# One level of Strassen for the projections of a two-branch token mixer on one TensorE

## The chip, the core and the metric

The kernel runs on one core of a Trainium2 chip, which has five engines with queues of their own: TensorE (PE, matrix products), VectorE (DVE), ScalarE (ACT), GpSimd (POOL) and SyncE (SP, which here only issues transfers). The metric is the device time of one execution in microseconds (us), the median over the runs.

## What is computed

One layer over 1024 tokens of width 1024, all in float32:

```python
h = rms_norm(x, pre_norm)
q, k, v, gate_a, u_b, v_b, gate_b, mg_a, mg_b = split(h @ w_in)   # 1024, 128, 128, then six of 1024 columns
o_a = sliding_window_attention(q, k, v, sinks, rel_bias)          # window 128, 16 heads, 2 K/V heads
y_a = (o_a * silu(gate_a)) @ w_branch_a
o_b = spatial_gating(gelu(u_b), gelu(v_b), ...)                   # layer norm of v, then tril(W) over chunks of 128
y_b = (o_b * silu(gate_b)) @ w_branch_b
merged = sigmoid(mg_a) * y_a + sigmoid(mg_b) * y_b
x = x + rms_norm(merged @ w_out, post_norm)
```

## The kernel before

**Products.** Every operand of a large product is held as a high part (rounded to the reduced float32 format fp32r, by ScalarE) and a low part (the rest, by a subtraction on GpSimd or VectorE). A product is the sum of three: high x high, high x low, low x high. `products` (from L460) lists them for one unit: 8 slabs of depth, 3 combinations, 2 halves of 512 columns, so 48 matmuls of 128x512, all issued at L474. A unit yields 128 output rows (features) x 1024 tokens in one of the two accumulators acc0 and acc1 (two PSUM banks each).

**Stages.** (1) The V branch: eight tiles of tokens; x is normalised, transposed, split and multiplied by the 1024 columns of v_b; GELU, layer norm and the chunk mix (L501, L503) follow, and mix_b goes to memory. h itself, transposed and split, is gathered in ht_hi and ht_lo. (2) U and gate_b, 16 units in turn, whose results make g_hi and g_lo. (3) merge gate B and branch B, 16 units. (4) K and V. (5) Attention: for each of eight head pairs the units gate_a, merge gate A and the next Q (144 matmuls) run, and `beside` puts a slot of attention work between them after every 11 matmuls (FIRST_SLOT, SLOT_STEP): scores of block k (L600), transpose of the probabilities of block k-2 (L612), values of block k-4 (L627). (6) Branch A, 8 units, with the merge. (7) The output: 8 tiles of tokens x 2 halves x 24 matmuls (L694), then the post norm, x added, and the store.

**What sets the order.** Each engine has its program in one written order, with semaphores between them. Loads of weight slabs are issued by SP (`load_raw`, L293) once the slab before the last is split; ScalarE makes w_hi (`split_hi`, L735), GpSimd w_lo (`split_lo`, L1015), and the unit waits for it. In attention VectorE takes for block k: masked copy of the scores (L1351), maxima over scores plus bias (L1357), the negated maximum and the sink's difference (L1363, L1364); ScalarE takes the exponentials (L912, L914); VectorE the denominator (L1339, L1340); GpSimd scales the probabilities (L1113) and masks their transposes (L1123). GpSimd also writes the bias row (L1092), which SP stores to memory and spreads to skew_d.

Of the kernel before, what the change touches and what calls it, by code (L numbers as in the profile page):

```python
# [5 lines left out]
P = 128  # L31
D_MODEL = 1024
SEQ = 1024
# [11 lines left out]
PAIRS = N_HEADS // 2  # L45
PAIRS_PER_KV = PAIRS // N_KV


# [11 lines left out]
N_U = NT  # L60
N_MB = N_U + 2 * KT
N_KVU = N_MB + 2 * KT
N_ATT = N_KVU + 2
N_YA = N_ATT + 3 * PAIRS
N_OUT = N_YA + KT
BIAS_ROW = 3 * P
WARM_UP = 24
UNIT = 6 * KT


FIRST_SLOT, SLOT_STEP, SLOTS = 19, 11, NT + 4
# [12 lines left out]
class Chain:  # L84


    def __init__(self, eng, sem):
        self.eng, self.sem, self.base, self.k = eng, sem, 0, 0

    def link(self, ins):  # L90
        self.k += 1
        ins.then_inc(self.sem, 1)
        self.eng.wait_ge(self.sem, self.base + self.k)

    def at(self, base):
        self.base, self.k = base, 0


def build(nc, x, rel_bias, pre_norm, post_norm, w_in, sinks, sgu_ln_g, sgu_ln_b,
          w_spatial, b_spatial, w_branch_a, w_branch_b, w_out, out):  # L100
    f32 = mybir.dt.float32
    f32r = mybir.dt.float32r
    bf16 = mybir.dt.bfloat16
# [8 lines left out]

    mix_d = nc.dram_tensor("mix_d", [KT, P, SEQ], f32)
    acc_d = nc.dram_tensor("acc_d", [KT, P, SEQ], f32)
    sig_d = nc.dram_tensor("sig_d", [KT, P, SEQ], f32)
# [3 lines left out]
    with ExitStack() as ctx:  # L119
# [6 lines left out]

        ht_hi = sb("ht_hi", [P, KT * SEQ], f32r)
        ht_lo = sb("ht_lo", [P, KT * SEQ], f32r)
        g_hi = sb("g_hi", [P, KT * SEQ], f32r)
        g_lo = sb("g_lo", [P, KT * SEQ], f32r)  # L130
        raw = [sb(f"raw{b}", [P, 1024]) for b in range(2)]
        w_hi = [sb(f"w_hi{b}", [P, 1024], f32r) for b in range(2)]
        w_lo = [sb(f"w_lo{b}", [P, 1024], f32r) for b in range(2)]
        buf_t = sb("buf_t", [P, SEQ])
        buf_a = sb("buf_a", [P, SEQ])
        buf_b = sb("buf_b", [P, SEQ])
        junk = sb("junk", [P, SEQ], bf16)
# [21 lines left out]
        bias_row = sb("bias_row", [N_HEADS, BIAS_ROW])  # L159


        with ExitStack() as s0:
            x_b = [sb(f"x_b{b}", [P, D_MODEL], f32, s0) for b in range(2)]
            pre_b = sb("pre_b", [P, D_MODEL], f32, s0)
            lng_b = sb("lng_b", [P, D_MODEL], f32, s0)
            lnb_b = sb("lnb_b", [P, D_MODEL], f32, s0)
            bs_b = sb("bs_b", [P, KT * P], f32, s0)
            mix_b = [sb(f"mix_b{b}", [P, KT * P], f32, s0) for b in range(2)]
            vn_hi = sb("vn_hi", [P, D_MODEL], f32r, s0)
            vn_lo = sb("vn_lo", [P, D_MODEL], f32r, s0)  # L170
            ws_st = sb("ws_st", [P, KT * 2 * P], f32r, s0)
        with ExitStack() as s1:
            k_hi = sb("k_hi", [P, N_KV * SEQ], f32r, s1)
            k_lo = sb("k_lo", [P, N_KV * SEQ], f32r, s1)
            v_st = sb("v_st", [P, N_KV * NT * P], f32r, s1)
            q_st = [sb(f"q_st{h}", [P, SEQ], f32r, s1) for h in range(2)]


            prob = [sb(f"prob{b}", [P, 256], f32, s1) for b in range(3)]
            pt_packed = sb("pt_packed", [P, 512], f32r, s1)  # L180
            pt = [sb(f"pt{b}", [P, 1024], f32r, s1) for b in range(2)]
            bias_t = sb("bias_t", [P, 512], f32, s1)
            bias_p = sb("bias_p", [P, 256], f32, s1)
            o_tmp = [sb(f"o_tmp{b}", [P, 256], f32, s1) for b in range(2)]
        with ExitStack() as s2:
            wo_hi = sb("wo_hi", [P, KT * HALF], f32r, s2)
            wo_lo = sb("wo_lo", [P, KT * HALF], f32r, s2)
            x_r = [sb(f"x_r{b}", [P, D_MODEL], f32, s2) for b in range(2)]
# [4 lines left out]
        ps_s, ps_p = ps_t[:, 0:512], ps_t[:, 512:768]  # L193

        raw_in = [sem(f"raw_in{b}") for b in range(2)]
        hi_done, lo_done = sem("hi_done"), sem("lo_done")
        unit_done = sem("unit_done")
        acc_free = [sem(f"acc_free{b}") for b in range(2)]  # L200
        x_in = [sem(f"x_in{b}") for b in range(2)]
        pre_in, ln_in, bs_in, wsp_in = sem("pre_in"), sem("ln_in"), sem("bs_in"), sem("wsp_in")
        rel_in, sink_in, bias_out, skew_out = sem("rel_in"), sem("sink_in"), sem("bias_out"), sem("skew_out")
        bias_made = sem("bias_made")
        const_ok, wsp_ok = sem("const_ok"), sem("wsp_ok")
        ssq_ok, msq_ok, rstd_ok, h_ok = sem("ssq_ok"), sem("msq_ok"), sem("rstd_ok"), sem("h_ok")
        tr_done = sem("tr_done")
        hs_hi, hs_lo = sem("hs_hi"), sem("hs_lo")
        ht_in = [sem(f"ht_in{b}") for b in range(2)]
        vb_in = [sem(f"vb_in{b}") for b in range(4)]  # L210
        vb_lo_dve, vb_lo_pool = sem("vb_lo_dve"), sem("vb_lo_pool")
        wsh_ok, wsl_ok = sem("wsh_ok"), sem("wsl_ok")
        var_ok, lnr_ok, vn_ok = sem("var_ok"), sem("lnr_ok"), sem("vn_ok")
        vnh_ok, vnl_ok = sem("vnh_ok"), sem("vnl_ok")
        mix_done, mix_lo_out, mix_ok, mix_biased = sem("mix_done"), sem("mix_lo_out"), sem("mix_ok"), sem("mix_biased")
        mix_out = [sem(f"mix_out{b}") for b in range(2)]
        mix_in, gate_t_ok, um_ok, prod_ok = sem("mix_in"), sem("gate_t_ok"), sem("um_ok"), sem("prod_ok")
        ghi_ok, g_ready = sem("ghi_ok"), sem("g_ready")
        spill_out = sem("spill_out")
        khi_ok, klo_ok, vt_done, vhi_ok = sem("khi_ok"), sem("klo_ok"), sem("vt_done"), sem("vhi_ok")  # L220
        bias_in, before_ok = sem("bias_in"), sem("before_ok")
        q_hi_ok = sem("q_hi_ok")
# [4 lines left out]
        pt_done, pth_ok, ptl_ok, pt_ok, pv_done = (  # L227
            sem("pt_done"), sem("pth_ok"), sem("ptl_ok"), sem("pt_ok"), sem("pv_done"))

        otmp_ok, oadd_ok, gtan_ok, og_ok = (  # L230
            sem("otmp_ok"), sem("oadd_ok"), sem("gtan_ok"), sem("og_ok"))
        siga_ok = sem("siga_ok")

        sigr_in, accr_in, mrg_ok, mhi_ok = sem("sigr_in"), sem("accr_in"), sem("mrg_ok"), sem("mhi_ok")
        post_in, xr_in = sem("post_in"), [sem(f"xr_in{b}") for b in range(2)]
        mt_hi, mt_lo = sem("mt_hi"), sem("mt_lo")

        osq_ok, oms_ok, ors_ok, y_ok = sem("osq_ok"), sem("oms_ok"), sem("ors_ok"), sem("y_ok")
# [29 lines left out]

        def wo_land(s):
            return raw[s % 2] if s < 6 else x_r[s % 2]  # L270

        def wait_wo(eng, s):

            if s in (5, 7):
                eng.wait_ge(wo_lo_dve, 1 if s == 5 else 2)
            else:
                eng.wait_ge(lo_done, N_OUT + (s if s < 5 else 5) + 1)

        def wait_vb_lo(eng, k):

            if k in vb_by_pool:
# [1222 lines left out]
```

## Time and profile before

| | us |
|---|---|
| median of 3 runs (1043.58 to 1044.3) | 1044.2 |
| span of the profiled execution | 1041.6 |
| TensorE busy | 1014.4 (97%) |
| VectorE, ScalarE, GpSimd busy | 459.4, 343.1, 402.0 |
| mean granted clock of TensorE | 0.995 |

The profile shows one execution on the chip. "Busy" is the time in which an engine worked on an instruction. PE is TensorE's matmuls, PEld its loads of the stationary operand, which run beside them. In a group of instructions "out<-in" names the tiles, "xcount" how many there are, then the busy time in us, the mean ns of one, and the idle time of the engine just before them with its releaser. Matmuls overlap in the pipeline, so their pace is read from the distance between starts, not from the duration of one. In rows cut into 40 slices each digit is tenths of a slice.

### The profile page before, as it was taken

The numbers are of one execution on the slowest core, as the hardware profiler recorded it, in microseconds if no ns is written. First come the engines' busy times: TensorE is split into PE (matmuls) and PEld (weight loads), VectorE is DVE, ScalarE is ACT, GpSimd is POOL, SyncE is SP. The second block draws the span as 40 slices with busy tenths as digits, with TensorE's granted clock in tenths as the row PEclk, the third lists the DMA queues.
The fourth block names the chain that finished last, engine by engine and source line by source line (L and its number), as shares of the span: only waits on it lengthen the run. The fifth ranks groups of instructions, "written<-read, shape, count | busy, mean of one in ns | idle before, by whom it ended". The sixth has DMA issues, their size and how long they took to land.

```text
span 1041.6 us, 14172 instructions
## 1 busy us (share of the span) xinstructions
PE 1014.4 (97%) x4792; PEld 840.5 (81%) x4792; DVE 459.4 (44%) x975; ACT 343.1 (33%) x716; POOL 402.0 (39%) x426
## 2 busy tenths in 40 slices
PE   7999999999999999999999999999999999999997
PEld 6888887888888888888877878787787878888886
DVE  6777633322331010011465566656556664335323
ACT  5333322212221111112354455455444533223221
POOL 2244545211212222122256656565565663224000
PEclk8999999999999999999999999999999999999999
DMA  9844242232531212212111112111111213455322
GB/s 314 230 143 141 84 133 87 69 92 60 154 89 60 81 60 92 69 60 81 31 52 62 52 40 70 40 53 49 61 51 41 71 42 101 163 212 174 137 81 81
DMA packets 113028, 98.03 MB, mean 94 GB/s; under 512 B 3664, under 2 KB 100960, under 8 KB 112992
## 3 DMA queue, kind: packets, MB, share of 16 engines
q1 hardware_dynamic: 108384, 80.79, 25.7%
q10 hardware_dynamic: 4608, 16.78, 4.2%
q8 instruction: 21, 0.34, 0.2%
q14 instruction: 15, 0.12, 0.0%
HBM read 72.36 MB, written 19.95 MB: 89 GB/s over the span
## 4 chain that ended last, share of the span: by engine, by line
PE 61%; DVE 13%; issue 13%; ACT 7%; POOL 3%; DMA 2%; DVEq 0%; ACTq 0%; SPq 0%; POOLq 0%
PE acc L474 56%; DVE neg_max L1363 3%; ACT prob L912 3%; DVE prob L1357 3%; DVE ps_t L1351 2%; PE ps_m L627 1%; DMA raw<-in_w_in 1%; DVE denom L1339 1%; ACT pt_packed L895 1%; ACT w_hi L875 1%; POOL bias_row L1092 1%; ACT buf_t L885 1%; ACT q_st L856 1%; PE ps_t L600 1%; DVE q_st L1318 1%
## 5 line engine op out<-in xcount | busy, mean ns | idle before, releaser
L1015 POOL TENSOR_TENSOR w_lo<-raw,w_hi 128x1024 fp32r<-128x1024 f32 x66 | 159.1, 2411 | 314.0 <-ACT w_hi L735 313.0
L474 PE MATMUL acc<-ht_hi,w_hi 128*128 128x512 f32 x800 | 250.7, 391 | 1.6 <-POOL w_lo L1015 1.6
L474 PE MATMUL acc<-ht_hi,w_lo 128*128 128x512 f32 x800 | 250.9, 392 | 0.0
L474 PE MATMUL acc<-ht_lo,w_hi 128*128 128x512 f32 x800 | 249.7, 390 | 0.0
L474 PEld LDWEIGHTS acc<-ht_hi,w_hi 128*128 128x128 f32 x800 | 149.1, 188 | 31.0 <-issue 2.0
L474 PEld LDWEIGHTS acc<-ht_lo,w_hi 128*128 128x128 f32 x800 | 149.4, 188 | 29.2
L474 PEld LDWEIGHTS acc<-ht_hi,w_lo 128*128 128x128 f32 x800 | 149.3, 188 | 29.2
L474 PE MATMUL acc<-g_hi,w_hi 128*128 128x512 f32 x384 | 120.3, 395 | 0.9 <-DVE w_lo L1192 0.5
L474 PE MATMUL acc<-g_lo,w_hi 128*128 128x512 f32 x384 | 119.4, 392 | 0.0
L474 PE MATMUL acc<-g_hi,w_lo 128*128 128x512 f32 x384 | 118.9, 391 | 0.0
L912 ACT ACTIVATE prob<-prob,neg_max 128x128 f32<-128x128 f32 x128 | 50.5, 395 | 151.6 <-DVE sink_d L1364 151.6
L735 ACT ACTIVATE w_hi<-raw 128x1024 fp32r<-128x1024 f32 x58 | 61.3, 1057 | 90.0 <-PE acc L474 78.5
L1113 POOL TENSOR_SCALAR prob<-prob,inv_den 128x128 f32<-128x128 f32 x128 | 46.0, 372 | 114.0 <-DVE inv_den L1340 114.0
L474 PEld LDWEIGHTS acc<-g_hi,w_hi 128*128 128x128 f32 x384 | 71.1, 189 | 17.8 <-DVE w_lo L1192 1.9
L474 PEld LDWEIGHTS acc<-g_hi,w_lo 128*128 128x128 f32 x384 | 72.1, 188 | 15.0
L474 PEld LDWEIGHTS acc<-g_lo,w_hi 128*128 128x128 f32 x384 | 71.9, 189 | 14.7
L1123 POOL TENSOR_SCALAR_AFFINE_SELECT pt<-pt_packed 128x512 fp32r<-128x512 f32 x120 | 73.5, 635 | 9.3 <-DVE pt_packed L1343 7.7
L600 PE MATMUL ps_t<-k_hi,q_st 128*128 128x256 f32 (+1 forms) x128 | 37.4, 315 | 6.0 <-DVE row_max L1357 5.1
L1363 DVE TENSOR_SCALAR neg_max<-row_max 128x2 f32<-128x2 f32 x64 | 41.2, 644 | 2.2
L1292 DVE TENSOR_TENSOR buf_a<-acc,buf_t 128x1024 f32<-128x1024 f32 x8 | 9.8, 1225 | 73.2 <-PE acc L474 73.2
L627 PEld LDWEIGHTS ps_m<-pt,v_st 128*128 128x128 f32 x240 | 37.6, 190 | 5.5
L1339 DVE TENSOR_TENSOR denom<-row_sum,sink_e 128x2 f32<-128x2 f32 x64 | 19.2, 300 | 50.9 <-ACT sink_e L914 50.9
(155 smaller groups left out, 1272.0 us busy)
## 6 DMA issues: line engine op xcount, KB each, us to landing
raw<-in_w_in SPq DMA_DIRECT2D x54, 512.0 KB, 3.8
x_b<-in_x SPq DMA_DIRECT2D x8, 512.0 KB, 5.1
ht_hi<-w_hi SPq DMA_DIRECT2D x8, 512.0 KB, 3.8
ht_lo<-w_lo SPq DMA_DIRECT2D x8, 512.0 KB, 4.8
mix_d<-mix_b SPq DMA_DIRECT2D x8, 512.0 KB, 3.3
buf_b<-mix_d SPq DMA_DIRECT2D x8, 512.0 KB, 3.3
raw<-in_w_branch_b SPq DMA_DIRECT2D x8, 512.0 KB, 3.5
acc_d<-buf_a ACTq DMA_DIRECT2D x8, 512.0 KB, 2.6
```

Of the source, the lines that this page charges most:

```text
L474: last = nc.tensor.matmul(o, l, r, start=a, stop=z, skip_group_check=True)
L600: last = nc.tensor.matmul(ps_s[:, h * 256 + lo:(h + 1) * 256], q_st[h][:, blk * P:(blk + 1) * P], kbuf[:, kc + lo:kc + 256], start=a, stop ...
L627: last = nc.tensor.matmul(o, v_st[:, v0:v0 + P], pt[blk % 2][:, c0:c0 + 256].rearrange("p (h c) -> p h c", h=2), start=(kb == kbs[0] and x ...
L735: nc.scalar.activation(w_hi[b][:, :] if dst is None else dst, raw[b][:, :], ACT.Copy).then_inc(hi_done, 1)
L912: nc.scalar.activation(w, w, ACT.Exp, bias=neg_max[:, 2 * k + h:2 * k + h + 1], accum_out=row_sum[:, 2 * k + h:2 * k + h + 1])
L1015: nc.gpsimd.tensor_tensor(w_lo[b][:, :], raw[b][:, :], w_hi[b][:, :].bitcast(f32), ALU.subtract).then_inc(lo_done, 1)
L1113: last = nc.gpsimd.tensor_scalar(w, w, inv_den[:, 2 * k - 2 + h:2 * k - 1 + h], 0.5, ALU.mult, ALU.mult)
L1123: last = nc.gpsimd.affine_select(out=pt[blk % 2][:, kb * 512:(kb + 1) * 512].rearrange("p (y q) -> p y q", y=4), in_=pt_packed[:, :].rearr ...
L1339: own.link(nc.vector.tensor_tensor(denom[:, m2], row_sum[:, m2], sink_e[:, m2], ALU.add))
L1351: own.link(nc.vector.copy_predicated(blocks(ps_s)[:, :, 1, :], heads(before_i), blocks(ps_s)[:, :, 0, :]))
L1357: last = nc.vector.tensor_tensor_reduce(out=prob[k % 3][:, cs], in0=ps_s[:, h * 256 + P:(h + 1) * 256], in1=bias, scale=HEAD_DIM ** -0.5, ...
L1363: nc.vector.tensor_scalar(neg_max[:, c2], row_max[:, c2], -1.0, None, ALU.mult)
```

## The change

The units of (2), (3) but branch B, and (5) become pairs: two slabs of 128 weight columns against all of h, as a 2x2 block product in Winograd's form of Strassen's scheme, seven products of 12 matmuls (4 slabs of depth x 3 combinations, 128x512) instead of eight. Branch B, branch A and the output projection come last, as whole 1024x1024 products in the same scheme, seven products of four units of 12 matmuls each. In outline:

- The sums of h for the scheme are made once behind the V branch (`t_sums`, `t_hi`, `t_lo`): h is kept in memory as ht_d, reloaded by halves, summed on VectorE, split by ScalarE and by GpSimd or VectorE, into `mv`, seven operands with high and low part. The third product of the first pair is the first to read them.
- For each pair VectorE makes four sums of the weights (`left_sums_1`, `left_sums_2`), ScalarE and GpSimd split 3584 columns in four parts instead of 2048, ScalarE evicts three partial results and VectorE adds three from PSUM (`c_11`, `c_22`, `c_21`); products 6, 5 and 3 go on in the bank of product 1, product 4 in that of 7, so they wait for the eviction before them.
- 24 pairs in this order: Q with gate_a and the two merge gates, by turns, 16 in all; then U with gate_b, 8. Attention of a head pair is spread over 14 products of two pairs, one slot in the middle of each product. Transposes come at slot k+3 and values at k+5. The values take the masked transposes of the block before against differences of V (`v_lo`, `pt_prev`), so GpSimd masks one tile per block and not two.
- K and V take their time from two banks behind the V branch, K goes to memory and half of it comes back for each K/V head. The LN gain and bias are folded into later steps (`row_weights`, `u_mix`).
- The squares: ScalarE makes the high parts of 128x2048 for both sides, GpSimd the left low part, VectorE the right low part, the sums and the results (`square`), with buffers for two operands of each side. The merge of the branches is on GpSimd, inside the square of branch B; the output's norm and x are done by rows of 128 while products 6, 5 and 3 of the last square run.

The diff, cut to what the prediction speaks of:

```diff
-        def unit(n, hn, b, rh, rl):
-            start_unit(n, hn, b)
-            run(products(b, w_hi[b], w_lo[b], rh, rl)).then_inc(unit_done, 1)
+FIRST_U, PAIRS = 16, 24
+STEPS = (2, 6, 7, 5, 1, 3, 4)
+ORDER = (1, 2, 7, 4, 6, 5, 3)
+def attention_at(n, s):
+    if not 1 <= n <= FIRST_U:
+        return None
+    return (n - 1) // 2, s + (0 if n % 2 else 7)
...
+# TensorE: one product of a pair
+for m in range(first, last):
+    k, y = m // 3, m % 3
+    ins = nc.tensor.matmul(bank, (w_lo if y == 2 else w_hi)[:, left + k * P:left + (k + 1) * P],
+                           right[:, (OPW if y == 1 else 0) + k * HALF:(OPW if y == 1 else 0) + (k + 1) * HALF],
+                           start=(m == 0 and x in (1, 2, 7)), stop=(m == 11), skip_group_check=True)
...
+# TensorE: a unit of a square
+if i == 0:
+    pe.wait_ge(ll_ok, f + 1)
+    pe.wait_ge(rl_ok, f + 1)
+if x == 7:
+    pe.wait_ge(c_ok, 12 * st + i + 1)
+if x == 4:
+    pe.wait_ge(p7_ok, 4 * st + i + 1)
...
+# VectorE, behind the V branch
+t_sums(0)
+ln_stats(NT - 1)
+ln_apply(NT - 1)
+mix_read(NT - 2)
+t_sums(1)          # waits for bias_out
+t_lo(1)
+nc.vector.tensor_tensor(k_tmp[1], acc[0], k_tmp[0], ALU.subtract)
+mix_read(NT - 1)
+t_sums(2)
+t_sums(3)
+t_lo(3)
+left_sums_1(0)
+left_sums_2(0)
...
+# VectorE, after slot s of pair n
+if s == 0:
+    c_11(n)
+    if n and kind(n - 1) == "Q":
+        gate_mul(n - 1, 0)
+if s == 1:
+    left_sums_1(n + 1)
+if s == 2:
+    left_sums_2(n + 1)
+if s == 3:
+    c_22(n)
...
+# VectorE, a square
+sum_t3(st)
+sum_t1(st)
+right_lo_square(f + 2)
+result(st, 11, 0)
+sum_t2(st)
+result(st, 11, 1)
+sum_t4(st)
+result(st, 11, 2)
+result(st, 11, 3)
...
+right_lo_square(f + 3)
...
+# GpSimd, the squares
+for f in range(21):
+    st, x = f // 7, ORDER[f % 7]
+    if 1 <= f < 20:
+        left_lo_square(f + 1)
+    for i in range(4):
+        if st == BRANCH_B and x in (2, 6, 5, 3):
+            merge({2: 11, 6: 21, 5: 22, 3: 12}[x], i)
...
+# SP, behind the V branch
+sp.wait_ge(bias_out, 16)
+sp.dma_start(skew_d[:, :, :], bass.AP(bias_d, 0, [[BIAS_ROW, N_HEADS], [0, P], [1, BIAS_ROW]]))
+sp.wait_ge(khi_ok, 1)
+sp.dma_start(k_d[0, :, :], k_tmp[0][:, :].bitcast(i32))
+spill_mix(NT - 1)
+load_pair(0, 0)    # waits for t_sums(2)
```

## Rows read from the trace of the kernel before

**Rows 1.** The page: busy us by engine, and TensorE's clock in 40 slices.

```profile
PE 1014.4 (97%) x4792; PEld 840.5 (81%) x4792; DVE 459.4 (44%) x975; ACT 343.1 (33%) x716; POOL 402.0 (39%) x426
...
PEclk8999999999999999999999999999999999999999
```

**Rows 2.** Groups of TensorE's large matmuls.

```profile
L474 PE MATMUL acc<-ht_hi,w_hi 128*128 128x512 f32 x800 | 250.7, 391 | 1.6 <-POOL w_lo L1015 1.6
...
L474 PE MATMUL acc<-g_lo,w_hi 128*128 128x512 f32 x384 | 119.4, 392 | 0.0
L694 PE MATMUL acc<-g_hi,w_hi 128*128 128x512 f32 x128 | 39.6, 391 | 0.0
...
L694 PE MATMUL acc<-wo_hi,w_hi 128*128 128x512 f32 x64 | 25.5, 398 | 0.0
```

**Rows 3.** Timeline of TensorE: start us, us, engine, line, operation, tiles.

```profile
399.99 0.62 PE L474 MATMUL acc<-g_lo,w_hi 128*128 128x512 f32 x2
...
409.51 0.62 PE L474 MATMUL acc<-g_lo,w_hi 128*128 128x512 f32 x2
...
1002.39 0.40 PE L694 MATMUL acc<-wo_hi,w_hi 128*128 128x512 f32 x1
...
1005.89 0.40 PE L694 MATMUL acc<-wo_hi,w_hi 128*128 128x512 f32 x1
```

**Rows 4.** Timeline at the end: the last matmul and the last store.

```profile
1035.36 0.39 PE L694 MATMUL acc<-g_hi,w_lo 128*128 128x512 f32 x1
...
1038.45 0.99 SPq L443 DMA_DIRECT2D out<-buf_b  x2
```

**Rows 5.** Windows: length, busy us (and instructions) by engine, clock, DMA share, GB/s.

```profile
497.40:947.00 449.60, 436.70 (x2170) 361.88 (x2169) 256.23 (x779) 195.91 (x545) 240.88 (x304) 1.00 0.23 74
```

**Rows 6.** Waits of TensorE's weight loads: us in total, times, longest.

```profile
PEld ps_t L600 <- DVE row_max L1357: 11.7, 24, 0.7
PEld ps_t L612 <- POOL prob L1113: 11.1, 16, 1.3
```

**Rows 7.** Groups of the other engines, by shape.

```profile
L1273 DVE TENSOR_TENSOR buf_a<-buf_a,buf_b 128x1024 f32<-128x1024 f32 x8 | 9.8, 1225 | 33.8 <-ACT buf_a L819 24.7 <-DMA buf_b<-mix_d 9.1
L1198 DVE TENSOR_TENSOR mix_b<-ps_m,mix_b 128x512 f32<-128x512 f32 x8 | 5.5, 691 | 13.3 <-ACT mix_b L757 13.3
L735 ACT ACTIVATE w_hi<-raw 128x1024 fp32r<-128x1024 f32 x58 | 61.3, 1057 | 90.0 <-PE acc L474 78.5 <-issue 10.6 <-DMA raw<-in_w_in 0.6
L875 ACT ACTIVATE w_hi<-raw 128x512 fp32r<-128x512 f32 x16 | 9.9, 616 | 0.0
L1015 POOL TENSOR_TENSOR w_lo<-raw,w_hi 128x1024 fp32r<-128x1024 f32 x66 | 159.1, 2411 | 314.0 <-ACT w_hi L735 313.0
L1363 DVE TENSOR_SCALAR neg_max<-row_max 128x2 f32<-128x2 f32 x64 | 41.2, 644 | 2.2
```

**Rows 8.** Timeline of GpSimd and VectorE where the two overlap.

```profile
878.69 2.40 POOL L1015 TENSOR_TENSOR w_lo<-raw,w_hi 128x1024 fp32r<-128x1024 f32 x1 [9.79 <-ACT w_hi L735]
878.71 1.23 DVE L1411 TENSOR_TENSOR buf_b<-acc,buf_t 128x1024 f32<-128x1024 f32 x1 [4.07 <-DMA buf_t<-sig_d]
...
880.05 2.13 DVE L1414 TENSOR_TENSOR buf_b<-buf_b,buf_a 128x1024 f32<-128x1024 f32 x1
```

**Rows 9.** Timeline of GpSimd, the bias row; then transfers: KB, us to landing.

```profile
158.41 9.92 POOL L1092 TENSOR_SCALAR bias_row<-rel_t 16x1 f32<-16x1 f32 x32
...
skew_d<-bias_d SPq DMA_DIRECT2D x1, 3072.0 KB, 15.7
...
bias_d<-bias_row SPq DMA_DIRECT2D x1, 24.0 KB, 3.0
```

**Rows 10.** Timeline of VectorE, one turn of the attention loop.

```profile
673.68 0.42 DVE L1351 COPY_PREDICATED ps_t<-before,ps_t 128x256 f32<-128x256 int32 x1
...
675.48 0.15 DVE L1364 TENSOR_TENSOR sink_d<-sink_p,row_max 128x2 f32<-128x2 f32 x1
...
676.67 0.16 DVE L1339 TENSOR_TENSOR denom<-row_sum,sink_e 128x2 f32<-128x2 f32 x1 [0.27 <-ACT sink_e L914]
...
677.40 0.42 DVE L1351 COPY_PREDICATED ps_t<-before,ps_t 128x256 f32<-128x256 int32 x1
```

More of the change, by code:

```diff
@@ L57, with phase, unit, kind @@
 MGB_COL = MGA_COL + D_MODEL
[L60 to L71, printed above, removed]
+FIRST_U, PAIRS = 16, 24
+U_ORDER = (0, 4, 1, 5, 2, 6, 3, 7)
+LEFT = {1: 0, 2: 1, 6: 2, 7: 3, 5: 4, 3: 5, 4: 6}
+RIGHT = {1: 0, 2: 1, 6: 2, 7: 3, 5: 4, 4: 5, 3: 6}
+STEPS = (2, 6, 7, 5, 1, 3, 4)
+ORDER = (1, 2, 7, 4, 6, 5, 3)
+BRANCH_A, BRANCH_B, OUTPUT = 0, 1, 2
+def phase(st, x):
+    return 7 * st + ORDER.index(x)
+def unit(st, x, i):
+    return 4 * phase(st, x) + i + 1
+def kind(n):
+    if n < FIRST_U:
+        return "M" if n % 2 else "Q"
+    return "U"
+def product_counts():
+    order = [(0, 1)]
+    for n in range(PAIRS):
+        order += [(n, 2), (n, 6), (n, 7), (n, 5)]
+        if n + 1 < PAIRS:
+            order.append((n + 1, 1))
+        order += [(n, 3), (n, 4)]
+    return {key: i + 1 for i, key in enumerate(order)}
+DONE = product_counts()
+def prep_counts():
+    count, out = 0, {}
+    for n in range(PAIRS):
+        for g in ((1, 2), (6, 7), (5, 3), (4,)):
+            count += 1
+            for x in g:
+                out[n, x] = count
+    return out
+SPLIT = prep_counts()
+L_K, L_V, L_T, L_PAIR = 0, 1, 2, 10
+def raw_count(load):
+    return 16 * len(range(load % 3, load + 1, 3))
 def bucket_runs():
@@ L172, in build @@
[L172 to L184, printed above, removed]
@@ L509, in vb_unit @@
+                ins.then_inc(mix_done, 1)
+            def vb_unit(t):
                 pe.wait_ge(hs_lo, t + 1)
[L510 to L521 removed]
@@ new lines, in _ @@
+            for t in range(2, NT):
+                vb_unit(t)
+            pe.wait_ge(kvl_ok, 1)
+            pe.wait_ge(gelu_ok[0], NT // 2)
+            kv_mms(0, k_w, 0, 12)
+            mix(NT - 2)
+            kv_mms(0, k_w, 12, 48).then_inc(k_done, 1)
+            pe.wait_ge(kvl_ok, 2)
+            pe.wait_ge(gelu_ok[1], NT // 2)
+            kv_mms(1, v_w, 0, 12)
+            mix(NT - 1)
+            kv_mms(1, v_w, 12, 48).then_inc(v_done, 1)
+            product(0, 1)
+            product(0, 2)
@@ L688, in out_half @@
-            def out_half(t, b, hf, ks=range(KT), first=False):
-                rh, rl = ((wo_hi, wo_lo) if hf == 0 else (g_hi[:, 0:KT * HALF], g_hi[:, KT * HALF:2 * KT * HALF]))
-                for k in ks:
-                    if first and k % 2 == 0:
-                        wait_wo(pe, 4 * hf + k // 2)
-                    for l, r, kind in ((w_hi[b], rh, 0), (w_hi[b], rl, 1), (w_lo[b], rh, 2)):
-                        last = nc.tensor.matmul(acc[b][:, hf * HALF:(hf + 1) * HALF], l[:, k * P:(k + 1) * P],
-                                                r[:, k * HALF:(k + 1) * HALF], start=(k == 0 and kind == 0),
-                                                stop=(k == KT - 1 and kind == 2), skip_group_check=True)
-                return last
@@ L1485 @@
+            u_gate(PAIRS - 1, 0)
+            for st in range(3):
+                square(st)
 INPUTS = ("x", "rel_bias", "pre_norm", "post_norm", "w_in", "sinks", "sgu_ln_g", "sgu_ln_b", "w_spatial",
```

2487 lines of the change are left out of this document (1488 added, 999 removed).

## Prediction

> **What bounds the kernel now.** I read the page's busy shares first: TensorE is busy for 1014.4 of 1041.6 us, at full clock in nearly every slice [rows 1]. The groups of lines then say with what: 3936 matmuls of 128x512 (800 and 384 in each of three combinations at L474, 384 at L694) [rows 2]. Their pace comes from the timeline: the pair at 399.99 and the pair at 409.51 us lie 42 matmuls apart, 0.2267 us each [rows 3]. 3936 x 0.2267 = 892 us, 86% of the span. The rest is small transposes and mixes, the head, the tail (last matmul issued at about 1035.5 us [rows 4]) and attention. For attention the window from the Q unit to the first output tile holds 449.6 us [rows 5]; it contains 1536 of the large matmuls, 348.2 us, so that attention with its waits costs 101 us. Of this the weight loads stood visibly idle for 22.8 us, waiting for VectorE's row maxima and GpSimd's probabilities [rows 6]. So the kernel is bound by TensorE's work, with one place, attention, where a loop through the other engines is about as long as TensorE's time for a slot.
>
> **What the change takes away.** 48 projection units of 48 matmuls (Q, both branch gates, both merge gates, U: 2304) become 24 pairs of seven products of 12 (2016). The last three projections (1152) become three squares of 7 x 4 x 12 = 336 each (1008). V branch, K and V stay. 3936 - 3504 = 432 matmuls go, 432 x 0.2267 = **97.9 us**. For the pace within a product, which stays in one bank with a new stationary tile each time, there are two rows: wo_hi and wo_lo run at (1005.89 - 1002.39)/15 = 0.233 us, the g_hi half with the same structure at 0.227 by its mean of 391 against 398 ns [rows 2, 3]. I take 0.227, since most groups show it; 0.233 for 3024 product matmuls would cost 20 us. Left alone, the change gives 1041.6 - 97.9 = 943.7 us.
>
> **What it adds on the other engines.** Durations of blocks that no row shows are estimates from two sizes of the same operation [rows 7]. VectorE takes 0.69 us for 512 columns and 1.225 for 1024, so 2.3 for 2048; ScalarE 0.62 and 1.06, so 1.9; GpSimd 2.41 for 1024, so 4.7 for 2048 and 1.25 for 512.
> A row decides how these add up. A GpSimd subtract from SBUF ran from 878.69 to 881.09 us. VectorE's product of acc (PSUM) and buf_t, begun at 878.71, took its usual 1.23; the next, of two SBUF tiles, begun at 880.05, took 2.13 and ended 1.09 after GpSimd let go [rows 8]. So a VectorE operation with two SBUF sources and a GpSimd operation run one after the other, never side by side. The added sums, right splits and gated results are nearly all of this kind. The Trainium skill (SBUF — State Buffer, "SBUF: two separate sides") says the same, that the pair of ports is locked for a whole instruction; by that rule the squares below can't be hidden, and without it my sum would be some 45 us lower; the trace agrees with the rule.
>
> **The seam before the pairs.** TensorE needs the Strassen sums of h for the third product. From the end of the V branch (0): GELU, statistics and the split of the last tile end at about 9.5 us (the copy of the mix stands in ScalarE's queue ahead of it). Then GpSimd writes the bias row, 32 instructions, 9.9 us [rows 9], and its store lands 3.0 us later: 22.4. VectorE's second group of sums waits for that store (t_sums(1), bias_out), and behind it in its queue stand t_lo, the low half of K, the last mix_read and t_sums(2): 2.8 + 1.9 (ScalarE) + 2.3 + 1.2 + 1.4 + 2.8 = 12.4, so 35. Only then is a slab free for the load of pair 0, and SP has put the 3 MB skew, 15.7 us [rows 9], ahead of it: 38 to 41. With ScalarE 1.1 and GpSimd 2.4 the first product starts at about 44, where K, V and two mixes end at 25.7. Some 5 us more go at product 6, which wants all four groups of sums. That is 23; bounds 5 (the bias row early, the skew beside other loads) and 30. I take **20 us**.
>
> **Pairs with attention.** A slot goes from 11 matmuls to 12, 2.72 us, plus 0.5 to 1.2 for attention itself. The loop from one copy_predicated to the next took 677.40 - 673.68 = 3.72 us before [rows 10]: scores, maximum, ScalarE's exponentials, denominator, the next slot. VectorE's queue now gets, between maximum and denominator, c_11 and gate_mul (slot 0), two sums (1, 2), and in slot 3 c_22, which waits for ScalarE's eviction of product 5. The gap there was 1.0 us [rows 10], filled by the exponentials. Two sums need 1.4; slot 3 needs 1.0 + 0.6 + 0.7 = 2.3, so that this loop is 5.0 against TensorE's 3.4. GpSimd has 7168 columns of split per head pair in place of three to five blocks of 1024, and blocks neg_max, whose mean of 644 ns already shows it [rows 7]. I count 1.5 us more waiting per head pair, 8 x 1.5 = **12 us** (-10 if the slot's 0.23 us of additional TensorE time pays for it, +30 if VectorE becomes the bound: of its 256 us in the window [rows 5], with the merges left out, 28 fall to a head pair, and 11 more come, 39 in TensorE's 48, most of it in the first of the two pairs). The U pairs hold 16.6 us of two-source and GpSimd work under 19.0 us of matmuls: nothing, and the one wait of 1.6 us at w_lo [rows 2] goes.
>
> **The squares.** A phase of 48 matmuls is 10.9 us, a square 76.2. Work that must take turns, per square: GpSimd 7 x 4.7 = 33; VectorE 15 x 2.3 = 34.5 (7 right splits, 8 sums) and 12 gated results, 8; 76 together, no reserve. Branch B adds 16 merges of 1.25 on GpSimd, 20; the output square 8 additions of x and 12 weighings, 18. So at least 0 + 20 + 18 less what lies in the tail, about 30. The order adds to it between products 7 and 4: after the right split for 7 VectorE must issue result, T2, result, T4, two results and the split for 4, 4 x 1.4 + 3 x 2.3 = 12.5, with GpSimd's 4.7 in between, 17 us in a phase of 10.9; and the units of product 7 wait for those results, as they share banks. In branch B the left split of 4 moreover stands in GpSimd's queue behind four merges. In the output square ScalarE's squares stand ahead of its next splits. Walked through phase by phase I get 12 us in branch A (10 at products 7 and 4, 2 at product 3, whose units wait for gated results), 19 in B (12 there, 3 at product 3, 4 at the next square's product 1) and 15 in the output square (4 at product 2, which waits for the last merges, 7 at 7 and 4, 4 at 3): **46 us** (bounds 15, if each wait hides in the buffers, and 75).
>
> **Ends.** Four row-weight matmuls, 1 us. From the last matmul to the end there are 6 us now [rows 4]; then a square, a mean, a root, two scaled rows and a store: 0.5 more. Removed multiplications by the LN gain, the mix bias and the spills lay beside matmuls: 0. In pauses as long as these the clock can fall to half; the only fall with work in it before is the head's slice (8 tenths) [rows 1], so I price it apart, 0 to 15 us, and take 0.
> Of this the Trainium skill (TensorE: Matmul & The Clock Gate, "HAM oscillation") says that such pauses let the clock fall; the trace before has none in mid-kernel, and the 15 us stand in the rival below.
>
> **Sum.** 943.7 + 20 + 12 - 1.6 + 46 + 1.5 = 1021.6 us of span. The measured median is 1044.2 where the profiled span is 1041.6, so 2.6 lie around it: **1024 us**.
>
> **Rivals.** (a) *TensorE stays the bound.* If work in buffers is far enough ahead, the squares cost 15, the seam 5, attention -5: 943.7 + 15 + 5 - 5 + 1.5 + 2.6 = 963; up to 1003. For it: each split is issued a phase ahead. Against: the turns above leave no reserve. (b) *Slower than before, through the turns on the shared port in the squares.* At 75 us there, with the clock at half after the pauses (up to 15) and seam and attention as forecast: 943.7 + 75 + 15 + 20 + 12 + 2.6 = 1068. It decides from squares and clock together at 64 us, where I have 46; one GpSimd block that wins the port in each phase ahead of VectorE's right split would do, 21 x 4.7 = 99 us less what was idle. (c) *Attention bound by VectorE*: +30 in place of 12, 1042, and no change.
>
> **How the numbers follow.** The forecast's own range is 1004 to 1041, chance 0.50; (a) 0.23; (b) 0.22; (c) or another sum that ends near zero, 0.05. Below 978 I leave 0.1, above 1056 0.1, so the range is 978 to 1056. A measurement here can tell 0.2% (2.1 us). Faster: 0.50 + 0.23 = 0.73; same 0.05; slower 0.22.
>
> **What would show it.** TensorE's large matmuls 3504, with PE's busy share falling to 90% or less. A pause of over 15 us before the first product 1 (about 125 to 170 us), ended by w_lo, and one at product 6. In the last 300 us waits of TensorE for right and left on VectorE and GpSimd, longest at product 7 and at product 4, and phases of 17 us where 10.9 stand alone. In attention waits as before, 22.8 us or up to 20 more. If PE's share stays at 96%, (a) holds and my walk through the queues is wrong; if the clock's row shows 5 to 8 tenths behind pauses, (b)'s second half is at work.

## The result, and the profile after

The changed kernel takes 1096.9 us (median of 4 runs, 1094.88 to 1101.38) where the kernel before takes 1044.0 (1043.58 to 1044.3): a ratio of 1.0515, 95% interval 1.0491 to 1.0539. It is 53 us slower; I had forecast 1024 us, 20 faster. The 432 matmuls are gone as planned, so the rest of the kernel costs some 150 us more, where I had written 78.

The page of the kernel after: its span, busy us by engine, and three engines and TensorE's clock in 40 slices.

```profile
span 1096.4 us, 12813 instructions
...
PE 950.5 (87%) x4364; PEld 776.7 (71%) x4364; DVE 768.0 (70%) x1306; ACT 482.4 (44%) x944; POOL 523.1 (48%) x415
...
PE   7999943998989898888888889999997996988884
...
DVE  5544453967767776777676766868678799688965
...
POOL 2233423454645555454555553545352448494435
PEclk8999976999999999999999999999998999899997
```

TensorE fell from 97% to 87%, VectorE rose from 44% to 70% [rows 1]. Three places stand out in TensorE's line: slices 6 and 7 (the seam), the long stretch of 8s and 9s (the pairs with attention), and the last ten (the squares and the tail). The profiled run took 1098.3 us against a span of 1096.4.

Windows of the kernel after, from the end of the K/V units to the first product, over the attention, and over the squares; columns as in rows 5:

```profile
148.50:178.60 30.10, 0.04 (x1) 0.00 (x0) 9.70 (x12) 5.61 (x6) 2.36 (x2) 0.54 0.84 267
210.00:660.00 450.00, 402.31 (x1968) 327.99 (x1967) 323.10 (x908) 231.30 (x639) 237.16 (x257) 0.98 0.25 78
801.30:1081.00 279.70, 246.47 (x1008) 198.38 (x1008) 226.01 (x137) 103.99 (x107) 145.48 (x46) 0.93 0.28 106
```

The second row answers to [rows 5]: an equal length, with 34 us less of TensorE and 67 us more of VectorE in it. In the third, 1008 matmuls at 0.2267 us would be 228.5 us. TensorE is busy with them for 246.5 at a granted clock of 0.93, and is idle for 33 us.

Waits of TensorE, us in total, times, longest:

```profile
PE acc L820 <- POOL w_lo L1470: 34.2, 2, 30.1
PE ps_t L848 <- DVE pt_pack L1720: 20.0, 8, 2.5
PE acc L978 <- issue: 14.5, 2, 9.3
PE ps_t L837 <- DVE row_max L1731: 13.8, 19, 1.6
PE acc L820 <- ACT ev L1119: 8.3, 8, 1.2
PE acc L978 <- DVE p L1854: 7.9, 5, 3.7
```

The first is the seam, in both of the places forecast. The third and sixth lie in the squares. The others lie in attention. The second and fifth are new there and regular: 8 times, once in each head pair. The fourth, for the row maxima, was there before with 5.1 us.

Where do they come from? The timeline of the kernel after (start us, us, engine, line, operation, tiles) at two places of one head pair, on GpSimd and VectorE around 331 us, and on GpSimd, VectorE and TensorE around 361 us (`ev<-acc,ev` is an addition that reads PSUM):

```profile
331.38 2.41 POOL L1470 TENSOR_TENSOR w_lo<-raw,w_hi 128x1024 fp32r<-128x1024 f32 x1 [4.87 <-ACT w_hi L1074]
...
331.85 1.96 DVE L1737 TENSOR_SCALAR neg_max<-row_max 128x2 f32<-128x2 f32 x1
...
360.97 2.42 POOL L1470 TENSOR_TENSOR w_lo<-raw,w_hi 128x1024 fp32r<-128x1024 f32 x1 [2.45 <-ACT w_hi L1074]
...
361.21 0.69 DVE L1665 TENSOR_TENSOR ev<-acc,ev 128x512 f32<-128x512 f32 x1
...
361.82 1.59 DVE L1715 TENSOR_TENSOR denom<-row_sum,sink_e 128x2 f32<-128x2 f32 x1
...
363.52 0.40 DVE L1720 TENSOR_TENSOR pt_pack<-ps_t,pt_pack 128x256 fp32r<-128x256 f32 x1
...
364.08 0.41 PE L848 MATMUL ps_t<-ident,prob 128*128 128x128 f32 x2 [2.50 <-DVE pt_pack L1720]
```

denom is an addition of two columns. It takes 1.59 us, because it begins while GpSimd splits 1024 columns and ends when that is through (363.4). Behind it in VectorE's queue stands pt_pack, and TensorE waits 2.5 us for that. At 331.85 the negated maximum is held in the same way for 1.96 us; the exponentials follow it on ScalarE, the eviction of product 6 follows them, and TensorE waits 1.0 us ahead of product 5. The long GpSimd operation thus reaches TensorE by way of VectorE's smallest operations. The addition at 361.21 reads one of its sources from PSUM and keeps its 0.69 us beside the same split.

### The profile page after: what moved, and what is told of

It reads as the page before. It is cut to its first block, busy times and chain, and to the rows that moved or that the text cites. A ratio compares the mean times of both kernels' runs of the same rounds, so it can differ in the third digit from the quotient of the medians.

```text
span 1096.4 us, 12813 instructions
## 1 busy us (share of the span) xinstructions
PE 950.5 (87%) x4364; PEld 776.7 (71%) x4364; DVE 768.0 (70%) x1306; ACT 482.4 (44%) x944; POOL 523.1 (48%) x415
## 4 chain that ended last, share of the span: by engine, by line
PE 37%; DVE 26%; issue 14%; ACT 12%; POOL 6%; DMA 4%; SPq 0%; DVEq 0%; ACTq 0%; POOLq 0%
PE acc L820 18%; PE acc L724 8%; PE acc L978 4%; DVE prob L1731 4%; ACT prob L1273 3%; DVE ps_t L1727 2%; POOL left L1474 2%; PE ps_t L978 2%; PE ps_m L978 2%; ACT w_hi L1088 2%; DVE denom L1715 1%; DVE neg_max L1737 1%; DMA raw<-in_w_in 1%; POOL acc_a L1480 1%; DVE ev L1665 1%
## 5 line engine op out<-in xcount | busy, mean ns | idle before, releaser
L820 PE MATMUL acc<-mv,w_hi 128*128 128x512 f32 x1344 | 430.1, 402 | 50.5 <-POOL w_lo L1470 34.2
L820 PEld LDWEIGHTS acc<-mv,w_hi 128*128 128x128 f32 x1344 | 249.3, 193 | 106.0 <-POOL w_lo L1470 34.8
L820 PE MATMUL acc<-mv,w_lo 128*128 128x512 f32 x672 | 266.6, 397 | 0.0
L1470 POOL TENSOR_TENSOR w_lo<-sums,w_hi 128x1024 fp32r<-128x1024 f32 x48 | 117.4, 2447 | 187.3 <-ACT w_hi L1088 112.3
L820 PEld LDWEIGHTS acc<-mv,w_lo 128*128 128x128 f32 x672 | 129.1, 192 | 28.4
L1470 POOL TENSOR_TENSOR w_lo<-raw,w_hi 128x1024 fp32r<-128x1024 f32 (+1 forms) x48 | 96.2, 2005 | 95.9 <-ACT w_hi L1074 92.5
L978 PE MATMUL acc<-right,left 128*128 128x512 f32 x432 | 109.2, 415 | 25.3 <-issue 14.5
L978 PEld LDWEIGHTS acc<-right,left 128*128 128x128 f32 x432 | 86.5, 202 | 47.7 <-issue 23.2
L978 PE MATMUL ps_t<-right,left 128*128 128x512 f32 x288 | 73.6, 415 | 9.7 <-POOL left L1474 5.2
L724 PE MATMUL acc<-mv 128*128 128x512 f32 x288 | 70.6, 400 | 1.2 <-DVE mv L1573 1.2
L1787 DVE TENSOR_TENSOR right<-g_a,right 128x2048 fp32r<-128x2048 f32 x12 | 44.1, 3673 | 10.6 <-ACT right L1231 10.5
L837 PE MATMUL ps_t<-k_hi,q_st 128*128 128x256 f32 (+1 forms) x128 | 37.2, 313 | 14.5 <-DVE row_max L1731 13.8
```

What stands on the lines that cost most here:

```text
L724: ins = nc.tensor.matmul(acc[b][:, hf * HALF:(hf + 1) * HALF], left, right, start=(m < 2), stop=(m >= 46), skip_group_check=True)
L820: ins = nc.tensor.matmul(bank, (w_lo if y == 2 else w_hi)[:, left + k * P:left + (k + 1) * P], right[:, (OPW if y == 1 else 0) + k * HALF: ...
L837: ins = nc.tensor.matmul(ps_s[:, h * 256 + lo:(h + 1) * 256], q_st[h][:, blk * P:(blk + 1) * P], kbuf[:, kc + lo:kc + 256], start=a, stop= ...
L978: ins = nc.tensor.matmul(bank, l[:, c:c + P], r[:, (OPW if y == 1 else 0) + k * HALF:(OPW if y == 1 else 0) + (k + 1) * HALF], start=(m == ...
L1470: nc.gpsimd.tensor_tensor(w_lo[:, c], src, w_hi[:, c].bitcast(f32), ALU.subtract).then_inc(wlo_ok, 1)
L1787: nc.vector.tensor_tensor(right[f % 2][:, OPW:2 * OPW], right_src(ORDER[f % 7]), right[f % 2][:, 0:OPW].bitcast(f32), ALU.subtract).then_i ...
```

## The experiments

All but the last ran once. Kernels that keep GpSimd's splits scatter: the kernel after itself spans 6.5 us in four runs, and the stretch from the first scores to the last values takes 443 to 452 us in the six kernels here that have its code untouched, at a granted clock of 0.98 to 0.96. I read less than 6 us between two single runs as nothing, unless the trace shows the place. The kernel before took 1043.07 to 1043.54 us beside them.

**no_attention.** `attend` is left out of every engine's loop, with its reloads of the bias, K and V.

> The whole attention loop is left out of the pairs on every engine, with its bias, K and V reloads, while the projections, the stores of the gates and the squares stay. Theory 1 (the attention costs 148 us where it stands, its own matmuls 75 and the rest its loop): 945 to 955 us, the pairs at the pace of the matmuls, 48 us for two pairs. Theory 2 (half of what I put on the attention is the pairs' own evictions and splits): 970 us or more, with waits for w_lo and for the evictions left in every pair.

Measured 948.5 us: theory 1. Attention where it stands costs 148 us, where I had read 101 before from [rows 5]. Without it the pairs run at the matmuls' pace, as a window of 410 us shows:

```profile
210.00:620.00 410.00, 407.56 (x1791) 337.11 (x1791) 220.57 (x236) 174.58 (x250) 198.51 (x87) 1.00 0.34 107
```

**pairs_short_lo.** Are the splits on GpSimd the cause?

```diff
+                if n:
+                    c, src = slice(c.start, c.start + 8), src[:, 0:8]
                 nc.gpsimd.tensor_tensor(w_lo[:, c], src, w_hi[:, c].bitcast(f32), ALU.subtract).then_inc(wlo_ok, 1)
```

> From the second weight pair on GpSimd makes only 8 columns of each low part of the weights' left factors in place of 512 or 1024, so this part of the computation is left out. Theory 1 (turns on the port shared by VectorE and GpSimd stretch the small operations of the attention loop): TensorE's waits for the lower half of the transposed probabilities (2.5 us a head pair) and for the eviction ahead of product 5 (1.0 us) go, 28 us in all and some clock: 1060 to 1072 us. Theory 2 (the order of VectorE's and ScalarE's queues alone sets the loop): at most 6 us, 1091 us or more.

Measured 1037.9 us, 59 less, twice what I had asked of theory 1. The windows from the first scores to the last values, in the kernel after and then in pairs_short_lo:

```profile
211.50:656.70 445.20, 397.51 (x1946) 324.07 (x1945) 321.63 (x906) 228.34 (x635) 235.48 (x256) 0.98 0.25 79
```

```profile
208.00:603.50 395.50, 379.98 (x1947) 319.63 (x1946) 264.49 (x905) 227.86 (x635) 105.95 (x254) 1.00 0.29 89
```

Of the 50 us, 32 are idle time of TensorE and 17.5 its busy time, which shrank as the clock rose from 0.98 to 1.00. The U pairs behind them take 7 us less. So 57 us hang on GpSimd's low parts. This run can't tell by which way they cost it, since it frees the port, GpSimd's queue and VectorE at once. Nor does it say how much of this is new: the kernel before has such splits beside its attention too, and no run leaves them out there.

**pairs_pieces** keeps the queue's work and shortens the holds.

```diff
+                w = (c.stop - c.start) if n == 0 else P
+                for d in range(0, c.stop - c.start, w):
+                    e = slice(c.start + d, c.start + d + w)
+                    ins = nc.gpsimd.tensor_tensor(w_lo[:, e], src[:, d:d + w], w_hi[:, e].bitcast(f32), ALU.subtract)
+                ins.then_inc(wlo_ok, 1)
```

> The kernel after, but from the second weight pair on GpSimd makes each low part in pieces of 128 columns, in 4 or 8 instructions in place of one: the same work in the same queue, and no hold of the port longer than one piece. Theory 1 (small operations of VectorE wait until a whole instruction of GpSimd is through): VectorE's operations of 1.6 and 2.0 us in the loop fall below 0.8 us, TensorE's waits of 2.5 us and 1.0 us shrink, 1070 to 1085 us. Theory 2 (GpSimd's queue is the cost: its scaling of the probabilities stands behind the low parts): no gain, 1094 us or more.

Measured 1097.2 us: the time is theory 2's, and yet theory 1's mechanism is there. The group of the negated maxima over 210 to 655 us (count, busy us, mean ns), first in the kernel after:

```profile
L1737 DVE TENSOR_SCALAR neg_max<-row_max 128x2 f32<-128x2 f32 x64 | 35.3, 551 | 2.2
```

The same group in pairs_pieces:

```profile
L1741 DVE TENSOR_SCALAR neg_max<-row_max 128x2 f32<-128x2 f32 x64 | 20.8, 324 | 2.2
```

And in pairs_short_lo:

```profile
L1739 DVE TENSOR_SCALAR neg_max<-row_max 128x2 f32<-128x2 f32 x63 | 10.7, 169 | 2.2
```

At the place of the 1.96 us it now takes 0.43, and TensorE's waits for pt_pack fell from 20.0 to 8.5 us, those for the eviction went. But a piece costs GpSimd 482 ns and more, eight of them 3.9 us where one instruction took 2.42, as the group of GpSimd's pieces over 210 to 660 us in pairs_pieces shows:

```profile
L1473 POOL TENSOR_TENSOR w_lo<-sums,w_hi 128x128 fp32r<-128x128 f32 x254 | 113.2, 482 | 76.7 <-ACT w_hi L1088 75.0 <-ACT w_hi L1081 1.7
```

New waits of TensorE took the place of the old ones, in the list of waits of pairs_pieces:

```profile
PE ps_m L867 <- POOL pt_prev L1511: 12.9, 8, 2.0
PE ps_t L848 <- DVE pt_pack L1724: 8.5, 8, 1.1
...
PE ps_t L848 <- POOL prob L1504: 6.9, 7, 1.1
```

So the hold of the port by a whole instruction is real: the waits that it made fell by 20 us. The second way, GpSimd's queue, in which the probabilities and the masks stand behind the split, ends waits of TensorE here (19.8 us), where the queue is longer; in the kernel after it ends none. How the 59 us divide is not settled.

**dve_lo_1, dve_lo_all.** One low part, or all four, go to VectorE. The new function of dve_lo_1, which runs in slot 1 where GpSimd had the split in slot 0:

```diff
+            def left_lo_1(n):
+                dve.wait_ge(whi_ok, SPLIT[n, 1])
+                nc.vector.tensor_tensor(w_lo[:, 0:1024], first_raw(n)[:, :], w_hi[:, 0:1024].bitcast(f32), ALU.subtract).then_inc(wl1_ok, 1)
```

> One of the four low parts of each weight pair, the one of 1024 columns for products 1 and 2, is made by VectorE (1.22 us) in place of GpSimd (2.4 us on the shared port), in the second slot of a pair. Theory 1 (this operation holds the port when the small operations of the loop want it, which makes the waits of 2.5 us and 1.0 us of a head pair): 1068 to 1080 us. Theory 2 (any work added to VectorE's queue costs the loop as much as the port gives back): 1090 us or more.

> All four low parts of each weight pair are made by VectorE (4.3 us a pair) and none by GpSimd (8.7 us a pair). Leaving them out altogether gave 1037.9. Theory 1 (the port was the cost, and VectorE, then 85% busy in the attention, has room): 1045 to 1065 us. Theory 2 (VectorE becomes the bound of the head pair): 1075 us or more, with TensorE's waits for row_max and the evictions grown.

Measured 1068.7 and 1066.0 us. Theory 1 for the first: the wait for pt_pack falls to 8.5 us, the one for the eviction goes. For the second, 1 us above theory 1's range. It says more by what it didn't give: moving the other three too bought 2.7 us, no more than the scatter, with the waits for row_max up from 13.8 in the kernel after to 18.3 us and those for pt_pack at 13.1. And yet in dve_lo_all neg_max is no longer held:

```profile
L1739 DVE TENSOR_SCALAR neg_max<-row_max 128x2 f32<-128x2 f32 x64 | 10.9, 170 | 2.2
```

From the first scores to the last values it takes 422.5 us, as in dve_lo_1 (422.9), where neg_max still has a mean of 331 ns. So the 50 us of pairs_short_lo fall into 23 that come back when VectorE does all the work, and 27 that come back only when the work is left out. This points to VectorE's own load as the next bound, as rival (c) had it.

**attn_order**, on top of dve_lo_1: ScalarE copies o_tmp ahead of the exponentials, VectorE takes bias_p behind the first block's maxima and c_21 a slot later. ScalarE's part:

```diff
-                if k < 8:
-                    exps(p, k)
                 if k >= 7 and k % 2:
 ...
+                if k < 8:
+                    exps(p, k)
```

> As dve_lo_1 (1068.7 us), and ScalarE copies the other head's outputs ahead of the exponentials, while VectorE makes the bias of the later blocks after the first block's maxima and the last sum of a Q or M pair in the slot after. Theory 1 (what is left of the waits of a head pair, 1.6 us for row_max at its second slot and 1.1 us for the probabilities at its tenth, is queue order on ScalarE and VectorE): 10 to 20 us less, 1049 to 1059 us. Theory 2 (what is left is the port again, by the other low parts of GpSimd): within 5 us of 1068.7.

Measured 1063.4 us, 5.3 less, between the theories and within the scatter. The waits of 1.1 us for pt_pack (8.5 us in all) are gone and the attention is 6 us shorter (422.9 to 416.7), but nine waits for VectorE's sums of results, 8.5 us, are new. That queue order was part of it is likely and not shown.

**seam_row, seam_order.** In seam_row the bias row is built in another buffer while the V branch runs, its two stores go out before most of the reload of h, and VectorE doesn't wait for them. seam_order moreover splits the sums of h ahead of the first weights. Two places of seam_row's edit:

```diff
-        bias_row = x_b[0][0:N_HEADS, 0:BIAS_ROW]
+        bias_row = c22[0:N_HEADS, 0:BIAS_ROW]
 ...
-                    dve.wait_ge(bias_out, 16)
```

> GpSimd builds the bias row in another buffer (c22) while the V branch still runs, VectorE's second group of sums no longer waits for its store, and the skewed copy is written ahead of the fourth load of the transposed h. Theory 1 (the gap before the first product is made by the bias row): VectorE's 12.3 us of waiting go, and with them the raw weights' load lands earlier; the first product starts at 155 to 165 us in place of 178.6 and the time is 1074 to 1084 us. Theory 2 (the gap is made by the reload of h and the sums and splits of it, the row only fills it): the first product starts no more than 5 us earlier, 1092 us or more.

> As seam_row (1088.1 us), and ScalarE and GpSimd make the parts of the transposed sums before the first weights' parts, for which ScalarE waited 15.5 us with the sums ready. Theory 1 (product 6 of the first pair waits at the end of that chain): product 1 starts up to 2 us later, product 6 some 7 us earlier, 1080 to 1083 us. Theory 2 (the reload of h through the memory sets it): within 2 us of 1088.

The timeline of the kernel after at the seam, on VectorE, ScalarE and TensorE:

```profile
142.26 3.52 DVE L1625 TENSOR_TENSOR pt_land<-raw 128x512 f32<-128x512 f32 x1 [12.28 <-DMA bias_d<-x_b]
...
175.10 1.06 ACT L1074 ACTIVATE w_hi<-raw 128x1024 fp32r<-128x1024 f32 x1 [24.49 <-DMA raw<-in_w_in]
...
178.64 1.22 PE L820 MATMUL acc<-mv,w_hi 128*128 128x512 f32 x2 [30.10 <-POOL w_lo L1470]
```

With the bias row early (1088.1 us), the timeline of seam_row has the same matmul at

```profile
165.77 1.22 PE L820 MATMUL acc<-mv,w_hi 128*128 128x512 f32 x2 [17.59 <-POOL w_lo L1472]
```

12.9 us earlier, as much as VectorE's 12.28 us of waiting; the time fell by 8.8, less than theory 1 had. In the 17.6 us of pause that are left stands, by the timeline, the reload of h: SP is busy with three of its loads from 127.4 to 144.2 us and with two more for 8.6 us. Behind them come VectorE's sums, and then the load of pair 0, which is issued at 154.3 us and lands at 162.2. No run shortens these. seam_order (1083.9 us) didn't do what theory 1 asked: product 6 stands at 177.74 us in place of 177.77, though its wait is down from 2.9 to 0.4 us. Product 1 begins 2.4 us later, and products 1 and 2 and a few transposes take 9.6 us, where 24 matmuls of 0.2267 are 5.4: for the first 5.3 us behind the pause the granted clock is 0.50. The 4.2 us between the two runs are within the scatter.

**squares_short_lo, squares_order, squares_dve_lo.** The same questions in the squares: GpSimd's split cut to 8 columns; product 4's right split ahead of S1 and S2; the split on VectorE.

```diff
+                right_lo_square(f + 3)
                 if st > BRANCH_A:
                     sum_s1(st)
                     sum_s2(st)
-                right_lo_square(f + 3)
```

> In the three squares GpSimd makes only 8 columns of each low part of the left factor in place of 2048 from the third product on, so this part of the computation is left out. Theory 1 (turns on the shared port make the squares' waits): of 35 us of waits and 18 us of lowered clock at most 20 stay: 1055 to 1067 us. Theory 2 (VectorE's queue, with five sums of 2048 columns ahead of the split that product 4 needs, makes them): the long waits before product 4 stay at over 5 us each, 1084 us or more.

> In the second and third square VectorE makes the low part of product 4's right factor ahead of the two sums for product 6 in place of behind them. Theory 1 (TensorE's waits of 9.3 us and 5.2 us before product 4 are VectorE's queue order): they fall by the two sums, 4.6 to 5.5 us each, and some clock with them: 1084 to 1090 us. Theory 2 (the wait moves to product 6, whose left factor needs the sums): 1094 us or more. Theory 3 (turns on the port make these waits, since both engines split 2048 columns there in 6.6 us each): 1094 us or more, with the waits before product 4 in place.

> In the squares all low parts of the left factor from the third product on are made by VectorE (2.3 us of 2048 columns when alone) in place of GpSimd (4.7 us). Leaving them out gave 1068.0. Theory 1 (the squares are bound by the time for which the shared port is taken: per product 4.7 us of GpSimd, 2.3 us of VectorE's split, 2.6 us of sums, 1.0 us of gates and 1.0 us of merges are 11.6 us against 10.9 us of matmuls, and 9.2 us when VectorE does both): 1072 to 1084 us. Theory 2 (VectorE's queue is the bound, now with 2.3 us more a product): 1097 us or more.

Measured 1068.0, 1093.5 and 1073.1 us. The timeline of the kernel after ahead of product 4 of branch B, on GpSimd, VectorE and TensorE:

```profile
925.04 6.57 POOL L1474 TENSOR_TENSOR left<-w_b,left 128x2048 fp32r<-128x2048 f32 x1
...
927.15 6.60 DVE L1787 TENSOR_TENSOR right<-g_a,right 128x2048 fp32r<-128x2048 f32 x1
...
933.86 2.47 PE L978 MATMUL acc<-right,left 128*128 128x512 f32 x5 [9.33 <-issue]
```

Two blocks that take 4.7 and 2.3 us alone take 6.6 each here: GpSimd's begins while VectorE is in a sum of two SBUF tiles that ends at 927.2, and VectorE's split ends 2.1 us behind GpSimd's. They take turns, and each duration holds the wait for the other. From the first matmul of the squares to the last it is 279.4 us, with the short splits 242.8, with VectorE's 253.6; the least is 228.5. So 37 of the 51 us over the least hang on GpSimd's split, and 26 come back although VectorE does it in full: theory 1 of both, the first 1 us above its range. Its time fell by 29 and not by 37, since the attention, untouched, took 7 us more in that run. The swap alone gave 3.4 us; its squares take 274.0 us, 5.4 less. In the timeline of squares_order the long wait stays, on the other engine:

```profile
931.24 13.19 PE L978 MATMUL acc<-right,left 128*128 128x512 f32 x48 [7.07 <-POOL left L1474]
```

The wait in the third square falls from 5.2 to 3.5 us, and one of 3.0 is new at product 6. This is nearest to theories 3 and 2: with the port taken, order is worth little.

**combo2, combo3, combo4.** combo2 is seam_order, attn_order and squares_dve_lo together; combo3 adds the swap and the last rows' order; combo4 the pieces.

```diff
                     for i in range(4):
                         out_mean(i, 12 + i + 1)
                         out_weigh(12, i)
-                        out_rows(i)
+                        if i:
+                            out_rows(i - 1)
+                    out_rows(3)
```

> The four edits together: the bias row early, the parts of h's sums ahead of the weights', the port freed of GpSimd's low parts in slot one of the pairs and in the squares, and the order of attn_order. If their gains add (13 of seam_order, 28 of dve_lo_1, 10 to 20 of attn_order, 13 to 25 of squares_dve_lo): 1011 to 1033 us, faster than the kernel before. If they meet the same wait or clock and don't add: 1045 us or more.

> As combo2 (1026.7 us), with the order of squares_order in the second and third square, and in the last rows VectorE takes the next mean and weighing ahead of a row's sum. Theory 1 (squares_order gave 3.4 us alone since the port then took the place of the queue; with the port free the waits of 6.3 and 2.5 us before product 4 go): 1016 to 1022 us, 1.8 us of it from the tail. Theory 2 (the splits of product 4 are late by ScalarE, not by VectorE's order): 1024 to 1026 us.

> As combo3, and GpSimd's remaining low parts in the pairs are made in pieces of 128 columns. Theory 1 (whole instructions of GpSimd still stretch the loop): 5 to 15 us below combo3. Theory 2 (the loop is left with queue order only, or the pieces cost GpSimd as much as they give): within 3 us of combo3 or above it.

> The kernel of combo3 again, timed in rounds beside the kernel before, for an interval: 1014 to 1018 us, a ratio of 0.971 to 0.976 to the kernel before, if its one look (1015.7 against 1043.1) was no accident.

Measured 1026.7, 1015.7 and 1023.0 us. The gains add: 13 + 33.5 + 24 = 70.5 from the kernel after, against 70.2 measured. The swap that shortened the squares by 5.4 us now shortens them by 9 (254.8 to 245.7), and the tail gives 2 (16.8 to 14.6): the waits ahead of product 4 go from 6.28 and 2.48 us to 1.87 and 0.66. The pieces cost 7 us. In four runs combo3 takes 1016.6 us (1015.24 to 1016.79) against 1043.1: a ratio of 0.9745, interval 0.9729 to 0.9761. It leaves nothing out and beats both kernels. The window of its squares, to be read against the third one above:

```profile
753.50:999.20 245.70, 233.08 (x1008) 190.17 (x1008) 207.17 (x156) 102.76 (x106) 44.49 (x26) 0.99 0.32 120
```

GpSimd is down from 145 to 44 us, VectorE is down as well, from 226 to 207, although it does GpSimd's splits on top, and the clock is back at 0.99.

## Why the prediction was wrong, step by step

- **The least, 943.7 us.** Right: the matmuls run at 0.2267 us where nothing makes them wait, and the terms below, as measured, account for the whole difference from it.
- **Seam, 20 us: 39.** The chain was right in each link and in its end (two waits, at products 1 and 6, with the bias row, its store and VectorE's wait in front). From 148.5 to 210.1 us lie 61.6 us with 22.8 us of matmuls and transposes. VectorE's part came as forecast: 12.4 us for the chain behind the bias row, 14.6 measured. Mis-sized was the load of pair 0 behind it: its buffer is free at 156.8 us, SP issues it at 162.35, behind other transfers that keep it busy, and it lands at 175.1, 18 us where I had 3 to 6. The half clock behind the pause adds 4. My own walk had given 23, and I rounded it down.
- **Attention, 12 us: 43.** This is the step that failed: 1.5 us of waiting per head pair, where more than 5 came. (From the first scores to the last values lie 445.2 us with some 1325 large matmuls, 300 us; that leaves 145, against 101. The run without attention gives 47, over the whole kernel.) I had the port rule from [rows 8], and the row that tells of it here: neg_max with a mean of 644 ns [rows 7], when 169 is what it takes undisturbed. I used it for a remark and counted the queues instead. The loop's small operations each begin while GpSimd may hold the port for 2.4 us, and two of them now end in a wait of TensorE. Rival (c) put +30 on VectorE's own load; the runs give 23 us back when GpSimd's splits go to VectorE and 27 more when they go altogether.
- **What stays open there.** The hold itself is not new. The mean of neg_max was higher before (644) than after (551), GpSimd was as busy in the window (240.9 and 237.2 us), and TensorE was idle for only 12.9 us of it [rows 5], now for 47.7. New are VectorE's 67 us more of work, and products that wait for evictions in the same queues. Why the same holds cost so much more in this order no run separates.
- **U pairs, -1.6 us: 7.** The low parts again; the stage falls from 144.7 to 137.8 us without the splits. A sum of turns that stays under TensorE's time is not free when order is fixed.
- **Squares, 46 us: 53.** Right in cause, turns on the port; near in size by luck. The waits, with 2 us ahead of the first product, are 35 us where I had walked to 46: 6.5 in branch A (forecast 12), 14 in B (19), 12.5 in the output square (15). The longest stood at product 4 (9.3 and 5.2 us), shorter ones at product 7. The other 18 us are clock, which I had priced apart at nothing.
- **Ends, 1.5 us: 10.6.** The last matmul ends at 1080.8 us, the kernel at 1096.4. Four rows of mean, root and scaling follow in turn, their means at 1081.9, 1086.8, 1089.1 and 1091.5 us, where I had counted one. The row-weight matmuls take 1.1.
- **Sum.** The misses, 19 + 31 + 9 + 7 + 9, are 75 us; the span missed by 1096.4 - 1021.6 = 74.8.
- **Rival (b)** named the mechanism and the sign, at 0.22, and put it in the wrong place: squares and clock stayed at 53, under its 64 us (66 by its own terms), the rest came through attention, where I let the port cost 1.5 us a head pair. The range ended at 1056 since each case behind it took one upper bound at a time. All four together, seam 30, attention 30, squares 75 and clock 15, give 943.7 + 150 - 1.6 + 1.5 + 2.6 = 1096 us, and three of them hang in part on GpSimd's splits.

## What to carry to other kernels

When a change tightens a latency loop on VectorE that has long GpSimd operations beside it, price each small VectorE operation of the loop at the length of the GpSimd operation that it can meet, and look in the trace for tiny operations with a mean far above their least. Such a mean says that there are holds, not what they cost: that depends on what waits behind them. Moving the split to VectorE takes half its time (1.22 us for 2.41) and ends the holds; in the squares the swap of the order paid more after that than before. Bounds that hang on one shared resource should be taken together.

## What was not expected of the hardware

- An operation of VectorE with one source in SBUF (neg_max, 2 columns, 0.17 us alone) is held by GpSimd as one with two is: up to 1.96 us. My rule from [rows 8] spoke of two sources only. A subtraction of 512 columns (q_st, 0.69 us) took 2.77 us on average over seven. Those that read a source from PSUM kept their 0.35, 0.42 and 0.69 us beside the same splits. The Trainium skill (SBUF — State Buffer, "SBUF: two separate sides") has the lock last for a whole instruction, and the traces agree.
- Cutting a GpSimd subtraction of 1024 columns into eight costs 3.9 us in place of 2.42.
- Seven pauses of TensorE of 2.8 to 9.3 us in the squares went with a granted clock of 0.93, 18 us on 228.5; in combo3, with pauses of 2.4 us and less and one of 6.8, it was 0.99. The Trainium skill (TensorE: Matmul & The Clock Gate, "HAM oscillation") says that pauses bring the clock down, and these traces agree.
